# Sample cross attention in four column groups, squares summed on VectorE, and another order in two stages of a decoder step

## The reference

```python
def memory_kv(mem, lp):
    mn = rms_norm(mem, lp["norm_mem"])
    mem_k = jnp.einsum("bmd,dhe->bmhe", mn, lp["w_mk"])
    mem_v = jnp.einsum("bmd,dhe->bmhe", mn, lp["w_mv"])
    return mem_k, mem_v

def cross_sublayer(x, mem_k, mem_v, lp):
    hn = rms_norm(x, lp["norm_x_pre"])
    q = jnp.einsum("bsd,dhe->bshe", hn, lp["w_xq"])
    s = jnp.einsum("bshe,bmhe->bhsm", q, mem_k).astype(jnp.float32) * MEM_SCALE
    p = jax.nn.softmax(s, axis=-1).astype(mem_v.dtype)
    o = jnp.einsum("bhsm,bmhe->bshe", p, mem_v)
    y = jnp.einsum("bshe,hed->bsd", o, lp["w_xo"])
    return x + rms_norm(y, lp["norm_x_post"])
```

## Time and profile before

| what | value |
|---|---|
| median of 3 runs | 1387.19 us (1385.79 to 1391.81) |
| profiled execution | 1388.81 us |
| its span | 1387.1 us |
| mean granted TensorE clock | 0.942 |
| busy: TensorE, VectorE, ScalarE, GpSimd | 89%, 63%, 46%, 19% |
| HBM | 209.31 MB read, 7.15 MB written |

### The profile page before, as it was taken

How to read it: one execution, slowest core, us unless ns; L and a number is a source line. 1 busy time by engine, 2 the same in 40 slices (tenths; PEclk the granted TensorE clock), 3 DMA queues, 4 the chain that set the end, 5 groups by cost and what they waited for, 6 DMA issues and landing times.

```text
span 1387.1 us, 25251 instructions
## 1 busy us (share of the span) xinstructions
PE 1230.3 (89%) x9712; PEld 1118.8 (81%) x9712; DVE 873.4 (63%) x1489; ACT 637.2 (46%) x1091; POOL 269.8 (19%) x346
## 2 busy tenths in 40 slices
PE   4889999998888999897779899999898889988883
PEld 4889999997666999784768899999786689988672
DVE  4688888788656234662377988888865733347514
ACT  5464444443554344542555445444453734445342
POOL 2200100102331233121411010101034213321230
PEclk8999999999998999899889999999999989999996
DMA  7754646546454566474357465656446546656701
GB/s 208 209 164 121 183 129 184 155 127 171 130 162 134 150 182 186 116 236 182 91 147 186 122 172 140 167 144 173 119 134 199 153 122 179 181 141 204 263 1 63
DMA packets 317545, 216.07 MB, mean 156 GB/s; under 512 B 21477, under 2 KB 300369, under 8 KB 316619
## 3 DMA queue, kind: packets, MB, share of 16 engines
q1 hardware_dynamic: 300624, 166.74, 43.6%
q0 software_dynamic: 16480, 47.73, 11.0%
q10 hardware_dynamic: 330, 0.11, 0.1%
HBM read 209.31 MB, written 7.15 MB: 156 GB/s over the span
## 4 chain that ended last, share of the span: by engine, by line
PE 53%; issue 17%; DVE 14%; POOL 8%; DMA 4%; ACT 3%; SPq 1%; POOLq 1%; ACTq 0%; DVEq 0%
PE U L662 10%; PE U L663 10%; PE U L664 9%; POOL ssq L552 7%; DVE wlo L1789 4%; PE U L678 2%; PE U L679 2%; PE HAB L781 2%; PE U L680 2%; DMA cp<-in_cache_kv_latent 2%; DMA stage<-in_w_in 1%; PE HAB L862 1%; PE HE L805 1%; PE HC L786 1%; PE HC L789 1%
## 5 line engine op out<-in xcount | busy, mean ns | idle before, releaser
L1789 DVE TENSOR_TENSOR wlo<-stage,whi 128x2048 fp32r<-128x2048 f32 x140 | 320.4, 2290 | 235.9 <-ACT whi L1239 221.9
L1239 ACT ACTIVATE whi<-stage 128x2048 fp32r<-128x2048 f32 (+2 forms) x159 | 274.7, 1730 | 338.6 <-PE U L664 278.3
L662 PE MATMUL U<-Ahi,whi 128*128 128x264 f32 (+1 forms) x1280 | 379.3, 296 | 38.3 <-DVE wlo L1789 27.5
L663 PE MATMUL U<-Alo,whi 128*128 128x264 f32 (+1 forms) x1280 | 371.3, 290 | 0.0
L664 PE MATMUL U<-Ahi,wlo 128*128 128x264 f32 (+1 forms) x1280 | 370.3, 289 | 0.0
L662 PEld LDWEIGHTS U<-Ahi,whi 128*128 128x128 f32 x1280 | 250.9, 196 | 40.3 <-DVE wlo L1789 29.1
L663 PEld LDWEIGHTS U<-Alo,whi 128*128 128x128 f32 x1280 | 250.7, 196 | 0.1
L664 PEld LDWEIGHTS U<-Ahi,wlo 128*128 128x128 f32 x1280 | 249.2, 195 | 0.0
L1941 DVE SCALAR_TENSOR_TENSOR acc<-uext,cwall,acc 128x256 f32<-128x256 f32 x464 | 188.5, 477 | 0.1
L552 POOL TENSOR_TENSOR ssq<-ssq,sqt 128x264 f32<-128x264 f32 x64 | 102.7, 1605 | 147.8 <-ACT sqt L1648 123.7
L662 PE MATMUL U<-Bhi,whi 128*128 128x264 f32 x384 | 109.0, 284 | 0.0
(11 more groups left out here) (414 smaller groups left out, 2285.5 us busy)
## 6 DMA issues: line engine op xcount, KB each, us to landing
stage<-in_w_in SPq DMA_DIRECT2D x76, 1024.0 KB, 5.8
stage<-in_w_out SPq DMA_DIRECT2D x32, 1024.0 KB, 6.1
stage<-in_w_mk SPq DMA_DIRECT2D x8, 1024.0 KB, 6.1
cp<-in_cache_kv_latent SPq DMA_DIRECT2D x64, 128.0 KB, 3.1
cp<-in_cache_kv_latent POOLq DMA_DIRECT2D x64, 128.0 KB, 3.1
stage<-in_w_mv SPq DMA_DIRECT2D x8, 1024.0 KB, 5.4
stage<-in_w_xq SPq DMA_DIRECT2D x8, 1024.0 KB, 5.6
Kt<-in_cache_mem_k POOLq DMA_DIRECT2D x16, 512.0 KB, 6.3
```

What stands on the lines that cost most here:

```text
L662: mm(bk[:, 0:cols], whi[:, s, w], hi[:, k, :], start=(k == 0), stop=False)
L663: mm(bk[:, 0:cols], whi[:, s, w], lo[:, k, :], start=False, stop=False)
L1239: return A_(out, in_, ACT.Copy, scale=scale)
L1789: ins = V.tensor_tensor(wlo[:, s, :], stage[:, s, :], whi[:, s, :].bitcast(F32), ALU.subtract)
```

## The change

- The samples' attention uses four column groups, one per head, of 8 columns each (`R` is 104 instead of 48): `qm` and `pm` get smaller, scores and values are products of one head, the values with 128 columns instead of 256.
- `dX` is no longer normalised before its transposes; the reciprocal becomes the scale of the copy `doX`. One transpose instead of two brings it back.
- `XO` is gone. ScalarE writes the upper half of a head's prompt columns from PSUM (`x_upper`), VectorE its lower half (`x_out`); of the sample columns both are made at the end.
- Key blocks 4 and 6 use banks `HA`, `HB` instead of `U`. The last head's transposes and values are moved behind them.
- The squares are added by VectorE (`add_squares`) from four `sqt` buffers, 14 adds; TensorE sums two tiles, `ssq` and the last `sqt`. The last block is squared before it is copied, and in the first half before the next weight split. GpSimd adds nothing. The `U_OUT` loops of ScalarE and VectorE are unrolled.
- In the memory-value stage each unit is cut in two with a row transpose in each gap; ScalarE and VectorE take another order to fit, and the lower half of unit `U_MV + 1` moves behind the reciprocal. Two waits for stores in `mem_out` go.
- At the layer change `partial`, `root` and `recip(1, rsx)` move behind the split of unit 2.

The core of the diff:

```diff
--- before.py
+++ after.py
...
-    sqt = at("sqt", [P, 2, T], W + 18944)
-    ssq = at("ssq", [P, T], W + 21056)
+    sqt = at("sqt", [P, 4, T], W + 21120)
+    ssq = at("ssq", [P, T], W + 25344)
...
-    XO = at("XO", [P, MH, T], W + 21120)
...
-    qm = at("qm", [P, 2, G, G + 1], W)
-
-    pm = at("pm", [P, 2, 2, NB, G + 1], W + 4352)
+    qm = at("qm", [P, MH, NB, NB], W)
...
+    def y_bank(b):
+        return (HA, HB) if b in (4, 6) else U
...
-            part(U_MV, 0, *MB, 0, 8)
-            sums(6, [ssq[:, :]], 4, lambda k: pe.wait_ge(ssq_add.sem, ssq_add.at(l, 16)))
-            part(U_MV, 0, *MB, 8, KC)
-            for r in range(2):
-                mem_rows(r)
-            unit(U_MV + 1, 1, *MB)
-            for r in range(2, 5):
-                mem_rows(r)
-            unit(U_MV + 2, 2, *MB)
-            mem_rows(5)
-            unit(U_MV + 3, 3, *MB)
-            mem_rows(6)
+
+            def squares(half):
+
+                sums(6 + 2 * half, [ssq[:, :], sqt[:, 3, :]], 4 + 2 * half,
+                     lambda k: pe.wait_ge(*((sq_last.sem, sq_last.at(l, half + 1)) if k else
+                                            (ssq_add.sem, ssq_add.at(l, 14 * half + 14)))))
+
+            part(U_MV, 0, *MB, 0, 4)
+            squares(0)
+            part(U_MV, 0, *MB, 4, KC)
+            mem_rows(0)
+            for i in range(1, 4):
+                part(U_MV + i, i, *MB, 0, 8)
+                mem_rows(2 * i - 1)
+                part(U_MV + i, i, *MB, 8, KC)
+                mem_rows(2 * i)
             pe.wait_ge(std.sem, std.at(l, 5))
             for q in range(4):
                 pe.wait_ge(h_lo.sem, h_lo.at(l, 9 + q))
                 part(U_XQ, 0, Bhi[:, :, :], Blo[:, :, :], 4 * q, 4 * q + 4)
                 pe.wait_ge(sq_rdy.sem, sq_rdy.at(l, 5 + q))
                 last = group([yg[:, 4 * q + c, :] for c in range(4)], q == 0, q == 3)
+                if q == 0:
+                    mem_rows(7)
...
+                elif b == 4:
+                    pe.wait_ge(xex.sem, xex.at(l, MH))
                 else:
-                    pe.wait_ge(kT_act.sem, kT_act.at(l, b))
-                    pe.wait_ge(kT_dve.sem, kT_dve.at(l, b))
+                    n = b if b < 4 else b - 1
+                    pe.wait_ge(kT_act.sem, kT_act.at(l, n))
+                    pe.wait_ge(kT_dve.sem, kT_dve.at(l, n))
...
-                    i, g = h // 2, h % 2
-                    k = NB * i + b
-                    q = qm[:, g, :, :].rearrange("p a c -> p (a c)")[:, k * G:(k + 1) * G]
-                    last = mm(ST[32 * g:32 * g + G, 0:NM], q, KTs[b % 2][:, h, :],
-                              start=(b == 0 and i == 0), stop=(b == NB - 1 and i == 1))
+                    last = mm(ST[32 * h:32 * h + NB, 0:NM], qm[:, h, b, :], KTs[b % 2][:, h, :],
+                              start=(b == 0), stop=(b == NB - 1))
...
-            x_transposes(3)
-            y_keys(4)
-            y_scores(3)
-            x_values(3)
-            for b in range(5, NB):
+            for b in range(4, NB):
                 y_keys(b)
                 y_scores(b - 1)
+            x_transposes(3)
             y_scores(NB - 1)
+            x_values(3)
...
-            wait_apart(pe, yp_rdy.sem, yp_rdy.at(l, 1))
+            wait_apart(pe, yex.sem, yex.at(l, 1))
...
-                last = tr(HC[:, t * R:(t + 1) * R], dX[:, t * P:(t + 1) * P], ident[0:R, 0:R])
+                last = tr(HC[:, t * P:t * P + R], dX[:, t * P:(t + 1) * P], ident[0:R, 0:R])
...
-                    for g in range(2):
-
-                        q = pm[:, t, g, :, :].rearrange("p b c -> p (b c)")[:, b * G:(b + 1) * G]
-                        v = Vt[b][:, t, :].rearrange("p (i g e) -> p g i e", g=2, e=MD)[:, g, :, :]
-                        last = mm(U[0][32 * g:32 * g + G, 0:2 * MD], q, v, start=(b + t == 0), stop=(b == NB - 1 and t == 1))
+                    for h in range(MH):
+                        last = mm(U[0][32 * h:32 * h + NB, 0:MD], pm[:, t, h, b, :], Vt[b][:, t, h * MD:(h + 1) * MD],
+                                  start=(b + t == 0), stop=(b == NB - 1 and t == 1))
...
+            tr(HC[:, 256:256 + R], doX[:, :], ident[0:R, 0:R]).then_inc(yoT_mm.sem, 1)
...
-            sums(8, [ssq[:, :]], 6, lambda k: pe.wait_ge(ssq_add.sem, ssq_add.at(l, 32)))
+            squares(1)
...
-                partial(l, 1)
-                root(stat.at(l, 1), l, rsq.at(l, 0), 1.0 / (32 * D))
...
+                if l and j == 0:
+                    partial(l, 1)
+                    root(stat.at(l, 1), l, rsq.at(l, 0), 1.0 / (32 * D))
...
+            def block_out(half, m, gain):
+
+                bk = U[m % 2][:, 0:T]
+                if m >= 4:
+                    act.wait_ge(ssq_add.sem, ssq_add.at(l, 14 * half + max(m - 4, 1)))
+                if m == 15:
+                    A_(sqt[:, 3, :], bk, ACT.Square).then_inc(sq_last.sem, 1)
+                    copy(yg[:, m, :], bk, par[:, gain + m:gain + m + 1]).then_inc(u_evac.sem, 1)
+                else:
+                    copy(yg[:, m, :], bk, par[:, gain + m:gain + m + 1])
+                    A_(sqt[:, m % 4, :], bk, ACT.Square).then_inc(u_evac.sem, 1)
+
+            for m in range(16):
+                step(U_OUT + m, m)
+                if m < 15:
+                    hi(U_OUT + m + 2, m)
+                block_out(0, m, G_POST)
+            hi(U_OUT + 17, 1)
...
-                for r in ((0, 1), (2, 3, 4), (5,), (6,))[s]:
-                    mem_out(r)
-                for q in ((), (0,), (1, 2), (3,))[s]:
-                    act.wait_ge(x_upd.sem, x_upd.at(l, q + 1))
-                    raw_upper(8, q, Bhi, G_XPRE, par)
-                    A_(yg[:, 4 * q:4 * q + 4, :], xT[:, 4 * q:4 * q + 4, :], ACT.Square).then_inc(sq_rdy.sem, 1)
+                mem_out((0, 2, 3, 5)[s])
+                if s == 2:
+                    mem_out(4)
+                act.wait_ge(x_upd.sem, x_upd.at(l, s + 1))
+                raw_upper(8, s, Bhi, G_XPRE, par)
+                A_(yg[:, 4 * s:4 * s + 4, :], xT[:, 4 * s:4 * s + 4, :], ACT.Square).then_inc(sq_rdy.sem, 1)
+                if s == 0:
+                    mem_out(1)
+                if s == 3:
+                    mem_out(6)
...
+            def x_upper(h):
+                act.wait_ge(xv_mm.sem, xv_mm.at(l, h + 1))
+                copy(XOhi[:, h, 0:TP], HE[:, 0:TP]).then_inc(xo_hi.sem, 1)
...
+            x_upper(0)
             x_move(1)
             x_probs(2)
...
+            x_upper(1)
...
-            y_keys(3)
+            x_upper(2)
+            for b in range(3, NB):
+                y_keys(b)
             x_move(3)
-            for b in range(4, NB):
...
+            x_upper(3)
+            root_table(6)
+            act.wait_ge(yr_rdy.sem, yr_rdy.at(l, 1))
             act.wait_ge(yo_mm.sem, yo_mm.at(l, 1))
-            copy(doX[:, :], U[0][0:R, 0:2 * MD]).then_inc(yo_ev.sem, 1)
-            act.wait_ge(yoT_ev.sem, yoT_ev.at(l, 1))
-            act.wait_ge(xv_ev.sem, xv_ev.at(l, MH))
-            root_table(6)
-            copy(XOhi[:, :, :], XO[:, :, :]).then_inc(xo_hi.sem, 1)
-            act.wait_ge(ssq_zero.sem, ssq_zero.at(l, 2))
+            copy(doX[:, :], U[0][0:R, 0:MD], sm[0:R, 11:12]).then_inc(yo_ev.sem, 1)
+            act.wait_ge(yoT_mm.sem, yoT_mm.at(l, 1))
+            copy(XOhi[:, :, TP:T], HC[:, 256:384].rearrange("p (h x) -> p h x", x=32)[:, :, 0:NB]).then_inc(xo_hi.sem, 1)
...
-                if bl >= 2:
-                    act.wait_ge(ssq_add.sem, ssq_add.at(l, 16 + bl - 1))
-                copy(yg[:, bl, :], U[bl % 2][:, 0:T], par[:, G_XPOST + bl:G_XPOST + bl + 1])
-                A_(sqt[:, bl % 2, :], U[bl % 2][:, 0:T], ACT.Square).then_inc(u_evac.sem, 1)
+                block_out(1, bl, G_XPOST)
...
-                recip(1, rsx)
...
+                if l and j == 0:
+                    recip(1, rsx)
...
+            def add_squares(half, m):
+
+                dve.wait_ge(u_evac.sem, u_evac.at(l, (U_OUT, U_XO)[half] + m + 1))
+                if m > 1:
+                    dve.wait_ge(ssq_add.sem, ssq_add.at(l, 14 * half + m - 1))
+                V.tensor_tensor(ssq[:, :], ssq[:, :] if m > 1 else sqt[:, 0, :], sqt[:, m % 4, :], ALU.add
+                                ).then_inc(ssq_add.sem, 1)
+
+            for m in range(15):
+                lo(U_OUT + m + 2, m)
+                if m:
+                    add_squares(0, m)
...
+            lo(U_MV + 1, 1)
             residual(0, 0)
             lo(U_MV + 2, 0)
+            residual(0, 1)
             raw_lower(8, 0, Blo, Bhi, G_XPRE)
-            residual(0, 1)
             lo(U_MV + 3, 1)
             residual(0, 2)
             raw_lower(8, 1, Blo, Bhi, G_XPRE)
+            lo(U_MV + 4, 0)
             residual(0, 3)
-            lo(U_MV + 4, 0)
...
-                dve.wait_ge(xv_mm.sem, xv_mm.at(l, h + 1))
-                V.tensor_copy(XO[:, h, 0:TP], HE[:, 0:TP]).then_inc(xv_ev.sem, 1)
+                dve.wait_ge(xo_hi.sem, xo_hi.at(l, h + 1))
```

(25 more changed lines are left out.)

85 lines of the change are left out of this document (16 added, 69 removed).

## The result

The changed kernel takes 1342.74 us (median of 4 runs, 1338.61 to 1345.96), the kernel before 1387.30 beside it (1385.79 to 1391.81). The ratio is 0.9666, with a 95% interval of 0.9635 to 0.9696. The profiled execution took 1344.54 us, its span is 1342.9: 44.2 us less than the span before, where 51.2 were forecast. The time lies inside the forecast range, 5.7 us above the forecast.

What follows compares the result with a forecast made beforehand. TensorE, busy 89% of the span, was taken as the bound, through its waits and the lowered clock behind them. Terms summed to 51.2 us off the profiled 1388.8, giving 1337.6; with the median 1.6 lower, 1337 was given, range 1329 to 1355.

Steps and rivals of the forecast that it cites:

- Memory-value stage: First value unit of memory to second query unit: 36.0 us against 48.4 and 49.3, a gain of 25.7 us.
- The walk through layer 0: Memory-value stage from 547.4 us: the sum's 2.32 us wait goes, a new 1.2 us wait comes before the second value unit.
- Rival A: Memory-value stage: VectorE takes over as the bound, TensorE stalls again, 4 us per layer, 1345 us; chance 17%.
- rival C: Memory-value stage: the clock does not come back, only 5.6 us gained per layer, 1352 us; chance 12%.
- Scores and exponentials: Samples' scores to the exponentials' transposes: 0.6 us less per layer for scores, 1.2 for the exponential path, 3.6 in all.
- Values: Samples' value products: 128 small products in four groups take 4.0 us per layer, gain 8.4 us, bounds -0.5 and +12.5.
- Rival B: Samples' value products: small products have a floor, values keep 8.1 us, 8.2 of 8.4 us missing, 1345 us; chance 12%.
- Tail to the output projection: Behind the last value product: 1.6 us with handovers instead of 4.26, gain 5.3 us, bounds 4 and 6.
- Output blocks and their sum: End of each layer: 2.8 us from the blocks' clock and 2.9 us from the shorter wait for the sum.
- Layer change: Between the layers: split moved into ScalarE's idle time, unit 4's weight issued 4 us earlier; gain 2.5 us, bounds 0 and 5.
- Rival D: Out-projection loops: VectorE's adds hold back the lower splits and lengthen each unit, 1388 us and above; chance 2%.
- two of my own signs of being wrong: Key-block wait longer than TensorE gained by then; layer-change wait for weights as long as before.

Runs made afterwards that it cites:

- yardstick: The changed kernel itself, unaltered, run again beside the last three follow-up kernels: 1341.06 us (6 runs), ratio 0.9652 to the kernel before.

## Why the prediction held, and where it did not

**Memory-value stage**, 25.7 forecast, 27.0 measured. The walk through layer 0 held step by step, and the clock too: 35.4 us at 1.00. The new wait before the second value unit is 0.45 us instead of 1.2: counted from the start of the stage, TensorE arrives 0.6 us later than in my walk and VectorE's split ends 0.2 us earlier. Rival A (VectorE bound) and rival C (clock stays low) are refuted by the two rows of the stage. My reason for the first 2.32 us was incomplete: I named the split ahead of the square and the add behind it as one chain, and to take away either suffices.

**Scores and exponentials**, +3.6 forecast, -2.3 measured (-1.1 in the yardstick's trace), below my bound of -0.3 per layer; the step that failed. It has two parts. The first is the transfer, which I had named and priced too low. From the start of the stretch to the last key block the changed kernel takes 0.5 and 1.0 us longer than the kernel before: its waits for keys are 2.0 and 2.2 us in layer 0, 0.5 and 3.3 in layer 1, where the kernel before waited 0.6 and 0.7. Layer 1 has 1.0 us of that already ahead of its first key block: a weight of the queries is issued there 1.5 us after the first of four key loads and takes 11.8 us to land, and TensorE waits 0.8 us behind it. The second is the way from the last key block to the transposes of the exponentials, where I booked 0.6 + 1.2 us less per layer. In layer 0 before, in the changed kernel, and with the keys first:

```profile
639.17:644.09 4.92, 3.02 (x25) 1.59 (x25) 1.75 (x5) 1.16 (x3) 0.00 (x0) 1.00 0.16 64
```

```profile
626.09:631.28 5.19, 5.19 (x32) 2.92 (x33) 1.27 (x3) 1.76 (x4) 0.00 (x0) 0.67 0.06 21
```

```profile
621.76:625.91 4.15, 3.90 (x33) 2.21 (x33) 1.27 (x3) 1.83 (x5) 0.00 (x0) 1.00 0.99 370
```

At a granted clock of 1.00 this way is 0.8 us shorter and not 1.8, since the last head's transposes and values, which I had moved behind the keys, now stand in it (32 or 33 instructions instead of 25), and the sum gave them no price. Behind the longer wait for the key the granted clock is 0.67, and the way is 0.3 us longer than before. This second loss does not come in every execution: in the yardstick's layer 0 the clock stays at 1.00 behind a wait of 2.25 us and the way takes 4.16. That keys share their queue with values is what makes them late, as the kernel with the keys first shows: its stretch is 4.9 and 5.5 us shorter.

**Values**, 8.4 forecast, 8.3 measured. The starts are 0.027 us apart on average (3.41 us for 128) against 0.031 assumed; that the row of the table still takes 4.3 us is due to the end of the last products and the copy. Rival B is refuted. The Trainium skill, TensorE: Matmul & The Clock Gate, Part 1, offers about 25 ns as the least distance from start to start and about 62 ns where the sequencer decodes each product. The second does not apply here. The average of 27 ns agrees with the first, but the four records of one round start 7 ns apart, below it.

**Tail to the output projection**, 5.3 forecast, 5.8 measured: right. From the end of the last value product it takes 1.4 us, where I had 1.6. My two terms counted 0.5 us of layer 1 twice, since its 7.6 us of value products already held the wait for the copy. **Output blocks and their sum**, 5.7 forecast, 7.9 measured: the blocks gained 2.0 instead of 1.4 per layer, because the whole 0.07 of clock came back; the sum gained 2.07 us in layer 0, where 2.0 were forecast (the last add does stay behind the split), and 1.8 instead of 0.9 in layer 1, where the whole wait for GpSimd went.

**Layer change**, +2.5 forecast, -1.5 measured (-0.2 in the yardstick's trace), outside the bound of 0; the second step that failed. I named the transfer of unit 4's weight as what is late next, and let its landing follow its issue. It does not. Counted from the start of GpSimd's own loads, the weight is issued 3.8 us after it instead of 8.4, and lands 20.5 us after it instead of 20.0 (issued 719.1, landed 730.7 before; 689.6 and 706.3 after). TensorE arrives earlier, the bytes do not, and the wait grows from 1.70 to 5.96 us. That these loads are the cause is shown by the kernel with late loads; that the new order by itself gains nothing, by the one with the old. The Trainium skill, DMA: Bandwidth & Descriptors, Issuing engines are not separate DMA queues, says that transfers started by different engines run on the same 16 DMA engines and interleave; the median of 11.9 us for SyncE's loads, 6.1 with GpSimd's moved away, agrees.

**The rest**, forecast as nothing, is -1.0: layer 1's attention takes 479.1 instead of 477.3 us, TensorE's waits for latent pages growing from 5.3 to 7.8 us. That this follows from the change is not shown: the kernels that leave this stretch as it is take 477.1 to 479.8 us, and the one with fifteen adds on GpSimd takes 475.4. The sentence "the gain made before is therefore carried on, as every transfer and every split there is triggered by TensorE's own progress", on the way to the sample attention, held in layer 0 and not in layer 1, where the query weight comes late. **Rival D** did not show; VectorE's adds do not lengthen a unit, as the stage behind the sixteen units starts at 546.8 us and before at 547.4.

In sum the local terms on TensorE, ScalarE and VectorE came to 49.0 us where 45.1 were forecast, and the three stretches with waits for transfers gave -4.8 where 6.1 were forecast. That is the whole gap of 7 us. So the time lies in the range although two of my own signs of being wrong came up, the longer wait for the last key block and the wait for weights in the layer change; that the local terms were 3.9 us better than booked was luck. The forecast itself was rounded up without a reason: 1337.6 less 1.6 is 1336.

## What to carry to other kernels

A gain ahead of a stretch that ends in a transfer should be booked as zero or less until the landing time has been followed to what shares the queue; order loads by first use, and keep large, late-needed loads out of stretches where weights are waited for. Small products should alternate between column groups. When two things are in a chain before a wait (a late square and a slow add), remove the one that costs less effort first and measure: the second may then cost nothing.

## What the runs showed of the hardware

- A GpSimd add of 128x264 takes 0.76 us alone and 2.21 us when it starts beside VectorE's 2.29 us split; both durations are in one trace, one instruction apart.
- Instructions of 128 columns start 0.109 us apart within one column group; going round four groups, four of them start in the same 0.109 us (128 within 12.59 and within 3.41 us), with the granted clock at 1.00 in both.
- A 1 MB weight load took a median of 11.9 us (three loads) beside 3 MB of other loads and 6.1 us (five loads) with these issued later. One of them was issued 4.6 us earlier than before, counted from the start of the other loads, and landed 0.5 us later.
- Behind a wait of 2.21 us for a key block the granted clock was 0.67 over the next 5.2 us in one execution of the changed kernel; behind a wait of 2.25 us at the same place it stayed at 1.00 in another.
